# Fourier tokens folded four ways, with the small token transform as one block before the first group's attention

## The chip, the cores and the metric

The kernel runs on one core of one Trainium2 chip. The metric is the device time of one execution in microseconds (us). Engines are PE (matmuls), DVE (vector), ACT (scalar), POOL (GpSimd) and SP (its queue issues loads). All data is float32.

## The reference, cut to what matters

One encoder layer on 1,024 tokens of 1,024 channels: layer norm, an input projection, then attention (8 heads) and a Fourier branch merged by sigmoid gates, an output projection, and a retrieval layer (PEER) that fetches 128 rows of each of two large tables for every token. The change touches the Fourier branch:

```python
zf = z.astype(jnp.float32).reshape(B, S, F_GROUPS, F_GROUP_DIM)
y = jnp.fft.fft2(zf, axes=(1, 3), norm='ortho').real
return y.astype(z.dtype).reshape(B, S, F_DIM) @ w_fourier
```

The real part is, for each of 4 groups, cos(tokens) times cos(channels) minus sin(tokens) times sin(channels), applied to z of 1,024 tokens by 128 channels.

## The kernel before, in words

The program is one straight list of instructions per engine, tied by semaphores written out by hand. A front end first makes, for all 1,024 tokens, the normalised rows (`h0_done`), their transposes, the latents (L374), the Fourier input `zT` (L383, evicted by ACT at L1007), the rotary key (L393), the keys (L414) and values (L422), and the transposed retrieval keys. Then the tokens go in 4 groups of 256. Each group has a front part, `front(g, m)`, a table of 256 steps m: 16 attention units (2 query tiles times 8 heads, one every 5 steps), gates (from m = 85), the output projection, a layer norm, 16 query products and the choice of experts; and a retrieval part, bound to the gathered rows. The front part of group 0 runs alone, before any row is gathered (`gather_u` waits for `handed`, which the choice of experts sets); that of groups 1 to 3 runs beside the retrieval of the group before. The order within a step is the order of the calls in the loops at the end of each engine's program.

An attention unit u on PE is: for the first query tile, the head's query product (L470, at m = 5u), which ACT copies (L1042) and DVE rotates (L760 to L763); the scores (L488, 5u+2) into `fA`; DVE's row maximum (L768); ACT's exponential (L1047); 8 transposes (L344, 5u+6), copied by DVE (L776); and the value products (L506, 5u+9). The scores of unit u+1 wait until the exponential of unit u has read `fA`.

The Fourier branch before is done so. `zc`: for 8 token tiles and 4 groups one product with [cos | -sin] of the channels, 128x256 each (L405), evicted in turn by DVE (L722) and ACT (L1014) into `zcs`; the column k = 512 of the token transform is made apart, as a sum over tiles (L726) times alternating signs (L440, `y_mid`). The token transform uses that the outputs k and 1024-k share their products, so 512 columns are made: `dft(m)`, called at each step of `front(0, m)`, issues at every odd m below 64 two 128x512 products (L598), accumulated over 8 token tiles in `acc`, with a 512 KB piece of the matrix `dft_seq` streamed through a ring of 4 by ACT's queue (L1029, L1136). After each 8 of them DVE joins the halves (L928 to L932) and ACT spills the result (L1141).

```python
            for m in range(STEPS):
                if has_slot(-1, m + LEAD, False):
                    peer(-1, m + LEAD)
                front(0, m)
                dft(m)
```

## Time and profile before

| | |
|---|---|
| runs | 3511.56 us median of 3 (3509.41 to 3511.76) |
| profiled execution | 3506.43 us, its span 3504.6 us |
| PE busy | 2694.9 us, 77% of the span |
| DVE, ACT, POOL busy | 2224.8, 1631.8, 2170.5 us |
| DMA | 1240.83 MB, mean 354 GB/s |
| chain that ended last | POOL 26%, DMA 26%, PE 16%, DVE 11%, issue 11% |

The shares are means over two different programs in one: a front end and a first group without gathers, up to about 610 us, and the retrieval after it, in which the DMA row of the page stands at 9 tenths and about 400 GB/s throughout. In rows that list time by order, the number in brackets is the idle time of the engine before the row and what ended it. An fp32 matmul is two instructions in the trace: `x4` for a pair of 128x512 products.

### The profile page before, as it was taken

Reading aid. Unit: us, or ns where it says so; the run is one execution under the profiler, and the core shown is the slowest. Engines: PE = TensorE matmul, PEld = TensorE weight load, DVE = VectorE, ACT = ScalarE, POOL = GpSimd, SP = SyncE. Lnnn points to the kernel's source line nnn. Section 1 sums busy time; section 2 is a strip of 40 time slices with the busy share of each in tenths; the row PEclk is TensorE's granted clock in tenths of the full one; section 3 lists DMA queues with packets and bytes.
Section 4 is the critical chain, followed back from the end, with each engine's and each line's share of the span. In section 5 each row is a group of like instructions: output and inputs, shape, how many; then the busy total and the mean of one; then the engine's idle time right before and its main releaser. Section 6 shows DMA issues by size and latency. Waiting matters only on the chain.

```text
span 3504.6 us, 40872 instructions
## 1 busy us (share of the span) xinstructions
PE 2694.9 (77%) x14008; PEld 2139.5 (61%) x14008; DVE 2224.8 (63%) x5012; ACT 1631.8 (47%) x1852; POOL 2170.5 (62%) x2075
## 2 busy tenths in 40 slices
PE   6999986677788777687887777777887777766676
PEld 3455755566676666576775666666766665555555
DVE  5143218668766678578766677677666785567753
ACT  1121102466554555465545555565555454445445
POOL 4000003777777766777777767777777667777775
PEclk9999998689899898789899986898998885566656
DMA  4224437999999999999999999999999999999998
GB/s 173 100 78 156 150 114 248 406 399 399 382 410 409 409 409 387 392 402 361 406 409 409 406 408 389 393 398 373 409 409 408 409 379 409 409 409 409 409 407 319
DMA packets 350433, 1240.83 MB, mean 354 GB/s; under 512 B 38481, under 2 KB 46161, under 8 KB 349713
## 3 DMA queue, kind: packets, MB, share of 16 engines
q0 software_dynamic: 294912, 1073.87, 77.9%
q1 hardware_dynamic: 34096, 117.94, 9.1%
q10 hardware_dynamic: 21216, 46.40, 3.7%
q8 instruction: 111, 1.82, 0.2%
q14 instruction: 98, 0.79, 0.1%
HBM read 1222.33 MB, written 15.73 MB: 353 GB/s over the span
## 4 chain that ended last, share of the span: by engine, by line
POOL 26%; DMA 26%; PE 16%; DVE 11%; issue 11%; DVEq 7%; ACT 3%; SPq 0%; ACTq 0%; POOLq 0%
POOL rows L322 14%; DMA rows<-in_peer_u,ids_peer 13%; POOL rows L313 13%; DMA rows<-in_peer_v,ids_peer 12%; DVE rows L889 3%; PE fA L530 2%; ACT av L1116 2%; PE mB L374 2%; PE acc L598 2%; PE acc L609 1%; PE fB L542 1%; PE mB L506 1%; PE fA L488 1%; DVEq L834 1%; DVEq L745 1%
## 5 line engine op out<-in xcount | busy, mean ns | idle before, releaser
L609 PE MATMUL acc<-ident,av 128*128 128x128 f32 x8192 | 1394.7, 328 | 683.6 <-ACT av L1116 672.0
L1116 ACT ACTIVATE av<-rows,coef 128x1024 f32<-128x1024 f32 x1024 | 1172.1, 1146 | 1298.8 <-DMA rows<-in_peer_v,ids_peer 1194.4
L609 PEld LDWEIGHTS acc<-ident,av 128*128 128x128 f32 x8192 | 1155.3, 170 | 938.7 <-ACT av L1116 881.2
L313 POOL DMA_INDIRECT rows<-in_peer_u,ids_peer x1024 | 1034.3, 1010 | 830.8 <-DVE ids_peer L860 353.0
L322 POOL DMA_INDIRECT rows<-in_peer_v,ids_peer x1024 | 1088.1, 1063 | 339.6 <-issue 257.2
L889 DVE CUSTOM_DVE_ANT_0 rows<-rows,fB 128x1024 f32<-128x1024 f32 x538 | 650.2, 1215 | 386.6 <-DMA rows<-in_peer_u,ids_peer 382.7
L889 DVE CUSTOM_DVE_ANT_0 rows<-rows,hh 128x1024 f32<-128x1024 f32 x486 | 590.9, 1222 | 329.6 <-DMA rows<-in_peer_u,ids_peer 323.1
L576 PE MATMUL mB<-hT_g,wring 128*128 128x256 f32 x1024 | 253.9, 405 | 1.1 <-ACT hT_g L1078 1.1
L530 PE MATMUL fA<-hT_g,wring 128*128 128x256 f32 x1024 | 237.7, 388 | 0.0
L576 PEld LDWEIGHTS mB<-hT_g,wring 128*128 128x128 f32 x1024 | 206.6, 207 | 31.1 <-ACT hT_g L1078 1.5
L530 PEld LDWEIGHTS fA<-hT_g,wring 128*128 128x128 f32 x1024 | 196.4, 196 | 25.9
L506 PEld LDWEIGHTS mB<-V,S 128*128 128x128 f32 x1024 | 139.1, 216 | 11.8 <-DVE S L776 6.1
L506 PE MATMUL mB<-V,S 128*128 128x64 f32 x1024 | 140.1, 297 | 3.5 <-DVE S L776 3.5
L488 PE MATMUL fA<-KT,hT_g 96*128 96x512 f32 x256 | 123.8, 606 | 4.9 <-issue 2.8
L1047 ACT ACTIVATE S<-fA,small 128x1024 f32<-128x1024 f32 x64 | 71.0, 1109 | 107.5 <-DVE small L770 76.9
L542 PE MATMUL fB<-yo,wring 128*128 128x256 f32 x512 | 115.8, 379 | 0.0
L1107 ACT ACT_TABLE_LOAD x83 | 106.5, 1283 | 1.5
L542 PEld LDWEIGHTS fB<-yo,wring 128*128 128x128 f32 x512 | 95.4, 190 | 12.0
L776 DVE COPY S<-fB 128x1024 f32<-128x1024 f32 x64 | 78.1, 1221 | 37.2 <-PE fB L344 36.0
L768 DVE TENSOR_REDUCE small<-fA 128x1 f32<-128x1024 f32 x64 | 78.1, 1220 | 22.1 <-PE fA L488 21.9
L889 DVE DVE_READ_ACCUMULATOR2_ANT dots<- 128x1 f32 x1024 | 84.1, 82 | 0.0
L344 PE MATMUL fB<-ident,S 128*128 128x128 f32 x512 | 80.4, 309 | 4.1 <-ACT S L1047 4.1
(158 smaller groups left out, 2130.3 us busy)
## 6 DMA issues: line engine op xcount, KB each, us to landing
wring<-in_wstream SPq DMA_DIRECT2D x192, 512.0 KB, 6.8
ln<-in_dft_seq ACTq DMA_DIRECT2D x32, 512.0 KB, 3.5
rows<-in_peer_u,ids_peer POOLq DMA_INDIRECT x1024, 11.1
rows<-in_peer_v,ids_peer POOLq DMA_INDIRECT x1024, 11.2
hT_g<-in_x SPq DMA_DIRECT2D x8, 512.0 KB, 3.7
hres_spill<-KT ACTq DMA_DIRECT2D x8, 512.0 KB, 2.7
hT_spill<-rows ACTq DMA_DIRECT2D x1, 4096.0 KB, 11.1
wring<-in_wstream SPq DMA_DIRECT2D x16, 256.0 KB, 6.1
```

Of the source, the lines that this page charges most:

```text
L313: pool.indirect_dma_start(u_rows[:, ring(g, i, NU), :], None, peer_u, bass.IndirectOffsetOnAxis(ap=ids_peer[:, t, s:s + 1], axis=0)).then_ ...
L322: pool.indirect_dma_start(v_rows[:, ring(g, i, NV), :], None, peer_v, bass.IndirectOffsetOnAxis(ap=ids_peer[:, t, s:s + 1], axis=0)).then_ ...
L344: return nc.tensor.transpose(out_, in_, ident[:, :])
L488: last = mm(fA[:, half * 512:(half + 1) * 512], qT_g[0:QK, h, tok(qt)], KT[0:QK, h, half * 512:(half + 1) * 512], start=True, stop=True)
L506: last = mm(m1[:, h * VD:(h + 1) * VD], probsT[:, tok(k)], V[:, k, h * VD:(h + 1) * VD], start=k == 0, stop=k == TT - 1)
L530: last = mm(gb[:, j * GROUP:(j + 1) * GROUP], w[:, tok(k)], hT_g[:, k, :], start=k == 0, stop=k == KD - 1)
L542: last = mm(yb[:, j * GROUP:(j + 1) * GROUP], w[:, tok(4 * j + k)], src[:, k, :], start=k == 0, stop=k == 3)
L576: last = mm(m0[:, (qc % 2) * GROUP:(qc % 2 + 1) * GROUP], w[:, tok(k)], hT_g[:, k, :], start=k == 0, stop=k == KD - 1)
L609: last = mm(acc[:, tok(k)], av[:, i % NAV, tok(k)], ident[:, :], is_transpose=True, start=i % SLOTS == 0 and k % 4 == 0, stop=i % SLOTS == ...
L889: v.tensor_tensor_reduce(out=row, in0=row, in1=h1, scale=1.0, scalar=0.0, op0=ALU.mult, op1=ALU.add, accum_out=dots[:, b, i % BATCH:i % BA ...
L1107: s.activation(act_out[:, k % 2, :], dots[:, k % 2, :], ACT.Gelu).then_inc(act_done, 1)
L1116: s.activation(av[:, i % NAV, :], v_rows[:, ring(g, i, NV), :], ACT.Copy, scale=coef[:, b, i % BATCH:i % BATCH + 1]).then_inc(scaled, 1)
```

## The change

The 1,024 tokens are folded four ways by symmetry: DVE adds and subtracts z at t and 1024-t, then at t and 512-t, so that four vectors of 256 tokens are left (even and odd outputs, cosine and sine). The channel products are then 32 of 128x128 (L408 after) instead of 32 of 128x256, and the token transform needs 8 products of 128x255 to 257 per group, plus one of a single row for token 256 (`mid_row`, L607 after), instead of 16 of 128x512. The matrix `dft_mat` is 1 MB, loaded once at the start by SP's queue; the 16 MB of `dft_seq` are no longer streamed. The transform is no longer called in the steps of the first group's attention but as a block ahead of it, with `acc` and `fA` in turn as output; ACT copies the sine part, DVE writes the four quarters of the output with strides of 2 and -2. PE waits for the last of them (`y_done`) before the attention, and ACT issues the loads of `ln` and waits for the spill (`y_spilled`) before its part of it.

```diff
@@ -146,11 +145,14 @@
         hT_all = rows[:, 0:KD, :]
-        zcs = hT_all.rearrange("p t (g c) -> p t g c", g=FG)
+        zcs = rows[:, KD:KD + 4, :].rearrange("p a (b n) -> p (a b) n", b=2)
         zT = hh
+        fold = S2[:, :, :, :].rearrange("p t c n -> p (t c n)").rearrange("p (g n) -> p g n", g=FG)
+        zx = hh.rearrange("p g (x n) -> p g x n", x=4)
...
-        dft_ring = ln[:, :, :].rearrange("p r (m n) -> p r m n", m=2)
+        dft_sb = ln[:, 2:4, :]
+        mid_sgn, mid_row = yo[0:1, 0, 0:EVEN], yo[0:1, 0, 512:1024]
...
-        cos_part, sin_part = acc[:, 0:512], acc[:, 512:1024]
+        dft_ps = (acc, fA)
...
             load(w_uv_sb, w_uv, w_kv_in)
             load(rope_all[64:128, :], rope_tab, rope_in)
+            load(dft_sb, dft_mat.rearrange("(h p) n -> p h n", p=P), dft_in)
...
@@ -394,15 +395,24 @@
 
-            for n in range(TT * FG):
-                tt, g = divmod(n, FG)
+            for n in range(2 * FG):
+                g, pair = divmod(n, 2)
+                pe.wait_ge(folded, g + 1)
                 if n == 0:
-                    pe.wait_ge(hT_in, 16)
-                if g == 0 or n == 0:
                     pe.wait_ge(z_sb, 2 * FG)
                 if positive(n - 3):
-                    pe.wait_ge(zc_sb[n % 2], n // 2 - 1)
-                mm(banks[n % 4][:, 0:2 * FD], zT[:, g, tok(tt)], dftc, start=True, stop=True).then_inc(zc_ps, 1)
+                    pe.wait_ge(zc_sb[n % 2], (n - 4) // 2 + 1)
+                for x in range(2):
+                    for half in range(2):
+                        o = (2 * x + half) * FD
+                        last = mm(banks[n % 4][:, o:o + FD], zx[:, g, 2 * pair + x, tok(half)],
+                                  dftc[:, pair * FD:(pair + 1) * FD], start=True, stop=True)
+                last.then_inc(zc_ps, 1)
+            pe.wait_ge(zc_sb[0], 3)
+            for g in range(FG):
+                last = mm(banks[0][0:1, g * FD:(g + 1) * FD], fold[:, g, HALFK:HALFK + 1], dftc[:, 0:FD],
+                          start=True, stop=True)
+            last.then_inc(zc_ps, 1)
 
             pe.wait_ge(w_kv_in, 32)
...
@@ -433,14 +443,9 @@
-            for e in range(2):
-                pe.wait_ge(zc_sb[e], TT * FG // 2)
-            pe.wait_ge(z_sum, 1)
-            for g in range(FG):
-                last = mm(m0[:, g:g + 1], zsum[:, g, :], altern[:, 0:1], start=True, stop=True)
-            last.then_inc(y_mid, 1)
-            pe.wait_ge(y_mid, 2)
-
+            pe.wait_ge(zc_sb[0], FG + 1)
+            pe.wait_ge(zc_sb[1], FG)
+            pe.wait_ge(dft_in, 16)
 
             def chunk(g, c):
...
@@ -587,16 +592,19 @@
             def dft(m):
 
-
-                if m % 2 == 1 and m < 2 * TT * FG:
-                    n = m // 2
-                    g, tt = divmod(n, TT)
-                    if tt == 0 and g > 0:
-                        pe.wait_ge(y_done, g)
-                    pe.wait_ge(dft_in[n % NDFT], 16 * (n // NDFT + 1))
-                    for cs, part in enumerate((cos_part, sin_part)):
-                        last = mm(part, zcs[:, tt, g, cs * FD:(cs + 1) * FD], dft_ring[:, n % NDFT, cs, :],
-                                  start=tt == 0, stop=tt == TT - 1)
+                g, step = divmod(m, DFT_PERIOD)
+                if g < FG and step == 1:
+                    if g > 1:
+                        pe.wait_ge(y_done, g - 1)
+                    ps_g = dft_ps[g % 2]
+                    for x, (first, count) in enumerate(((0, EVEN), (512, HALFK), (EVEN, HALFK - 1), (512 + HALFK, HALFK))):
+                        cols = slice(first, first + count)
+                        for half in range(2):
+                            o = (2 * (x % 2) + half) * FD
+                            last = mm(ps_g[:, cols], zcs[:, 2 * g + x // 2, o:o + FD], dft_sb[:, half, cols],
+                                      start=half == 0, stop=half == 1 and x > 0)
+                        if x == 0:
+                            mm(ps_g[:, cols], mid_row[:, g * FD:(g + 1) * FD], mid_sgn, start=False, stop=True)
                     last.then_inc(dft_used, 1)
...
+            for m in range(DFT_PERIOD * FG):
+                dft(m)
+            pe.wait_ge(y_done, FG)
             for m in range(STEPS):
                 if has_slot(-1, m + LEAD, False):
                     peer(-1, m + LEAD)
                 front(0, m)
-                dft(m)
             for g in range(GROUPS):
                 for m in range(STEPS):
...
@@ -698,6 +708,21 @@
             latents(TT - 1)
+
+            for g in range(FG):
+                dve.wait_ge(z_sb, 2 * g + 2)
+                z, a, b = zT[:, g, :], fold[:, g, 0:S // 2 + 1], fold[:, g, S // 2:S]
+                v.tensor_copy(a[:, 0:S // 2 + 1:S // 2], z[:, 0:S // 2 + 1:S // 2])
+                v.tensor_tensor(a[:, 1:S // 2], z[:, 1:S // 2], z[:, S - 1:S // 2:-1], ALU.add)
+                v.tensor_tensor(b[:, 1:S // 2], z[:, 1:S // 2], z[:, S - 1:S // 2:-1], ALU.subtract)
+                dve.drain()
+                v.tensor_tensor(zx[:, g, 0, :], a[:, 0:HALFK], a[:, S // 2:HALFK:-1], ALU.add)
+                v.tensor_tensor(zx[:, g, 1, :], a[:, 0:HALFK], a[:, S // 2:HALFK:-1], ALU.subtract)
+                v.tensor_tensor(zx[:, g, 2, 0:1], b[:, HALFK:HALFK + 1], b[:, HALFK:HALFK + 1], ALU.subtract)
+                v.tensor_tensor(zx[:, g, 2, 1:HALFK], b[:, 1:HALFK], b[:, S // 2 - 1:HALFK:-1], ALU.subtract)
+                v.tensor_copy(zx[:, g, 3, 0:1], b[:, HALFK:HALFK + 1])
+                v.tensor_tensor(zx[:, g, 3, 1:HALFK], b[:, 1:HALFK], b[:, S // 2 - 1:HALFK:-1],
+                                ALU.add).then_inc(folded, 1)
 
...
+            for n in range(0, 2 * FG, 2):
                 dve.wait_ge(zc_ps, n + 1)
-                v.tensor_copy(zcs[:, tt, g, :], banks[n % 4][:, 0:2 * FD]).then_inc(zc_sb[0], 1)
-
-            dve.wait_ge(zc_sb[0], TT * FG // 2)
-            dve.wait_ge(zc_sb[1], TT * FG // 2)
-            v.reduce_sum(zsum, zcs[:, :, :, 0:FD].rearrange("p t g c -> p g c t"), AX).then_inc(z_sum, 1)
+                v.tensor_copy(zcs[:, n, :], banks[n % 4]).then_inc(zc_sb[0], 1)
+            dve.wait_ge(zc_ps, 2 * FG + 1)
+            v.tensor_copy(mid_row, banks[0][0:1, :]).then_inc(zc_sb[0], 1)
             dve.wait_ge(stored, 16)
             for i in range(TT):
...
@@ -919,26 +938,30 @@
             def dft(m):
 
-                if m % (2 * TT) == 2 * TT - 1 and m < 2 * TT * FG:
-                    g = m // (2 * TT)
-                    dve.wait_ge(dft_used, TT * (g + 1))
+                g, step = divmod(m, DFT_PERIOD)
+                if g < FG and step == 3:
+                    dve.wait_ge(sin_sb, g + 1)
                     if g >= 2:
                         dve.wait_ge(y_spilled[g % 2], 16)
                     y = y_part[:, g % 2, :]
-                    v.tensor_copy(y[:, S // 2:S // 2 + 1], ymid[:, g:g + 1])
-                    v.tensor_copy(ybuf[:, 0:512], sin_part)
+                    cos_even, cos_odd = dft_ps[g % 2][:, 0:EVEN], dft_ps[g % 2][:, 512:512 + HALFK]
+                    even, odd = cos_even[:, 1:HALFK], cos_odd
+                    sin_g = ybuf[:, 512 * (g % 2):512 * (g % 2 + 1)]
+                    sin_even, sin_odd = sin_g[:, 1:HALFK], sin_g[:, HALFK:2 * HALFK]
+                    v.tensor_copy(y[:, 0:S // 2 + 1:S // 2], cos_even[:, 0:EVEN:HALFK])
+                    v.tensor_tensor(y[:, 2:S // 2:2], even, sin_even, ALU.add)
+                    v.tensor_tensor(y[:, S - 2:S // 2:-2], even, sin_even, ALU.subtract)
+                    v.tensor_tensor(y[:, 1:S // 2:2], odd, sin_odd, ALU.add)
+                    v.tensor_tensor(y[:, S - 1:S // 2:-2], odd, sin_odd, ALU.subtract).then_inc(y_done, 1)
                     dve.drain()
-                    v.tensor_tensor(y[:, 0:512], cos_part, ybuf[:, 0:512], ALU.add)
-                    v.tensor_tensor(y[:, S - 1:S // 2:-1], cos_part[:, 1:512], ybuf[:, 1:512],
-                                    ALU.subtract).then_inc(y_done, 1)
-                    dve.drain()
-
+
+            for m in range(DFT_PERIOD * FG):
+                dft(m)
             for m in range(STEPS):
                 if m == L0:
                     dve.wait_ge(ln_in, 64)
                 peer(-1, m, False)
                 front(0, m)
-                dft(m)
 
             def group(g, last):
...
@@ -1008,10 +1031,9 @@
             load_queries(0)
-            for n in range(1, TT * FG, 2):
-                tt, g = divmod(n, FG)
+            for n in range(1, 2 * FG, 2):
                 act.wait_ge(zc_ps, n + 1)
-                s.activation(zcs[:, tt, g, :], banks[n % 4][:, 0:2 * FD], ACT.Copy).then_inc(zc_sb[1], 1)
+                s.activation(zcs[:, n, :], banks[n % 4], ACT.Copy).then_inc(zc_sb[1], 1)
             act.wait_ge(kr_sb, 2)
             for n in range(H):
...
-            for n in range(NDFT):
-                act.dma_start(dft_ring[:, n, :, :],
-                              dft_seq[:, tok(n), :].rearrange("m p n -> p m n")).then_inc(dft_in[n], 16)
 
 
...
 
             def dft(m):
-                n = m // 2 - 1 + NDFT
-                if m % 2 == 0 and NDFT <= n < TT * FG:
-                    act.wait_ge(dft_used, n - NDFT + 1)
-                    act.dma_start(dft_ring[:, n % NDFT, :, :],
-                                  dft_seq[:, tok(n % TT), :].rearrange("m p n -> p m n")).then_inc(dft_in[n % NDFT], 16)
-                if m % (2 * TT) == 1 and 0 < m // (2 * TT) <= FG:
-                    g = m // (2 * TT) - 1
+                g, step = divmod(m, DFT_PERIOD)
+                if g < FG and step == 2:
+                    act.wait_ge(dft_used, g + 1)
+                    if g > 1:
+                        act.wait_ge(y_done, g - 1)
+                    sin_g = ybuf[:, 512 * (g % 2):512 * (g % 2 + 1)]
+                    sin_both = dft_ps[g % 2][:, :].rearrange("p (b n) -> p b n", b=2)[:, :, HALFK:512]
+                    s.activation(sin_g.rearrange("p (b n) -> p b n", b=2), sin_both, ACT.Copy).then_inc(sin_sb, 1)
+                if g < FG and step == 4:
                     act.wait_ge(y_done, g + 1)
                     act.dma_start(yT_d[:, g, :], y_part[:, g % 2, :]).then_inc(y_spilled[g % 2], 16)
-                if m == 2 * TT * FG + 2:
+                if m == DFT_PERIOD * FG:
                     for j in range(4):
...
 
+            for m in range(DFT_PERIOD * FG + 1):
+                dft(m)
             for m in range(STEPS):
                 if has_slot(-1, m + LEAD, False):
                     scale(-1, m + LEAD)
                 gelus(-1, m, False)
...
     rope = np.concatenate([cos, cos, -sin, sin]).astype(np.float32)
-    n = np.arange(S)
-    w = 2 * math.pi * ((n[:, None] * n[None, :]) % S) / S
-    dft_seq = np.stack([np.cos(w), np.sin(w)])[:, :, :S // 2].astype(np.float32)
+    n = np.arange(S // 4)
+    even, odd = np.arange(0, S // 2 + 1, 2), np.arange(1, S // 2, 2)
+
+    def turn(rows, cols):
+
+        return 2 * math.pi * ((rows[:, None] * cols[None, :]) % S) / S
+
+    sin_rows = np.r_[S // 4, 1:S // 4]
+    dft_mat = np.concatenate([np.cos(turn(n, even)), np.sin(turn(n, even[1:-1])), np.cos(turn(n, odd)),
+                              np.sin(turn(sin_rows, odd))], axis=1).astype(np.float32)
+    mid_sign = np.cos(turn(np.array([S // 4]), even)).astype(np.float32)
     c = np.arange(FD)
```

On PE, between the channel products and the second attention unit, the order before is (the name `hh` holds z, `keysT` the latents, `ln` the transform's matrix):

```order
L405 MATMUL fA<-av,hh 128x256 x2
L405 MATMUL fB<-av,hh 128x256 x2
L414 MATMUL mB<-keysT,ln 128x512 x16
L422 MATMUL mB<-ln,keysT 128x512 x16
L344 MATMUL mB<-ident,hT_g 128x128 x16
L440 MATMUL mB<-small,prod 128x1 x4
L470 MATMUL mB<-cqT_g,wring 128x256 x2
L598 MATMUL acc<-ln,rows 128x512 x2
L488 MATMUL fA<-KT,hT_g 128x512 x2
L598 MATMUL acc<-ln,rows 128x512 x2
L470 MATMUL mB<-cqT_g,wring 128x256 x2
L598 MATMUL acc<-ln,rows 128x512 x2
```

and of the change:

```order
L413 MATMUL fA<-av,S 1x128 x4
L424 MATMUL mB<-keysT,ln 128x512 x16
L432 MATMUL mB<-ln,keysT 128x512 x16
L345 MATMUL mB<-ident,hT_g 128x128 x16
L604 MATMUL acc<-ln,rows 128x257 x2
L607 MATMUL acc<-yo 128x257
L604 MATMUL acc<-ln,rows 128x256 x2
L604 MATMUL acc<-ln,rows 128x255 x2
L604 MATMUL acc<-ln,rows 128x256 x2
L604 MATMUL fA<-ln,rows 128x257 x2
```

The 32 pairs at L598 no longer lie between the attention's instructions; after the block (four times the last rows, on `acc` and `fA` in turn) L475, the query product, follows, and then scores, query product, transposes, scores and value products without anything between.

On ACT, at the end of the block, with the semaphores that it waits for, the order of the change is:

```order
L1159 ACTIVATE ybuf<-fA 128x512 [waits y_done,dft_used]
L1162 DMA yT_spill<-hh 128x1024 [waits y_done]
L1165 DMA ln<-in_lnp 128x1024 x4
L1061 ACTIVATE hT_g<-mB 64x256 [waits q_ps,y_spilled1,y_spilled0]
L1066 ACT_TABLE_LOAD
L1066 ACTIVATE S,rowsum<-fA,small 128x1024 [waits row_max]
```

The spill and the four `ln` loads now stand ahead of the first query copy (L1061), which waits for the spills. Before, they came at m = 65 and 66, behind 13 units.

## Rows read from the trace of the kernel before

**Rows 1.** Busy time by stage: stretch, length, busy us of each engine (instructions), clock, DMA, GB/s
```profile
235.00:358.00 123.00, 117.82 (x504) 71.54 (x504) 50.53 (x77) 20.07 (x35) 0.00 (x0) 0.99 0.45 150
358.00:378.00 20.00, 15.39 (x91) 11.69 (x88) 9.03 (x10) 3.61 (x6) 0.00 (x0) 0.91 0.81 261
378.00:510.00 132.00, 119.89 (x483) 92.61 (x482) 20.55 (x34) 12.00 (x23) 0.00 (x0) 0.94 0.42 128
...
620.00:3504.00 2884.00, 2172.46 (x12016) 1804.68 (x12013) 1977.23 (x4453) 1527.97 (x1642) 2085.68 (x2011) 0.82 1.01 398
```

**Rows 2.** Chain of work that ended last, 230 to 237 us: start, us, what
```profile
230.98 1.07 PE mB L440 x8
232.28 1.13 PE mB L470 x4
...
235.13 1.78 PE fA L488 x4
```

**Rows 3.** Order of time on PE: start, us, instruction, count, idle before it
```profile
182.25 1.13 PE L405 MATMUL fA<-av,hh 128*128 128x256 f32 x4
...
185.31 1.10 PE L405 MATMUL fA<-av,hh 128*128 128x256 f32 x4 [1.06 <-DVE rows L722]
...
197.47 13.90 PE L414 MATMUL mB<-keysT,ln 128*128 128x512 f32 x32
```

**Rows 4.** Order of time on PE, the last attention units of group 0
```profile
363.92 1.88 PE L488 MATMUL fA<-KT,hT_g 96*128 96x512 f32 x4
365.63 1.90 PE L506 MATMUL mB<-V,S 128*128 128x64 f32 x16
368.59 1.09 PE L344 MATMUL fB<-ident,S 128*128 128x128 f32 x8 [1.06 <-ACT S L1047]
369.51 1.88 PE L488 MATMUL fA<-KT,hT_g 96*128 96x512 f32 x4
...
374.18 1.93 PE L344 MATMUL fB<-ident,S 128*128 128x128 f32 x8 [1.05 <-ACT S L1047]
377.42 3.67 PE L506 MATMUL mB<-V,S 128*128 128x64 f32 x16 [1.31 <-DVE S L776]
```

**Rows 5.** Groups by line and shape, 235 to 358 us
```profile
L598 PE MATMUL acc<-ln,rows 128*128 128x512 f32 x125 | 60.2, 603 | 1.6 <-DVE hh L932 1.1 <-issue 0.5
```

**Rows 6.** Order of time on DVE, 28 to 251 us
```profile
28.28 1.29 DVE L646 BATCH_NORM_STATS2 st<-hT_g 128x6 f32<-128x512 f32 x2 [2.13 <-DMA hT_g<-in_x]
...
31.68 0.69 DVE L671 TENSOR_TENSOR V<-mB,KT 128x512 f32<-128x512 f32 x1 [1.59 <-PE mB L374]
...
175.59 0.75 DVE L711 SCALAR_TENSOR_TENSOR prod<-mB,small,yo 32x512 f32<-32x512 f32 x1 [62.80 <-PE mB L393]
...
184.73 0.42 DVE L722 COPY rows<-fA 128x256 f32<-128x256 f32 x1
...
198.15 7.22 DVE L726 TENSOR_REDUCE prod<-rows 128x512 f32<-128x4096 f32 x1 [0.49 <-ACT rows L1014]
...
249.92 0.42 DVE L760 TENSOR_TENSOR prod<-mB,rope_g 32x256 f32<-32x256 f32 x1 [4.63 <-PE mB L470]
...
250.86 0.42 DVE L763 TENSOR_TENSOR hT_g<-prod 32x256 f32<-32x256 f32 x1
```

**Rows 7.** Order of time on ACT and its queue
```profile
168.49 0.69 ACT L1007 ACTIVATE hh<-fB,small 128x512 f32<-128x512 f32 x1 [6.18 <-PE fB L383]
...
357.92 0.34 ACTq L1141 DMA_DIRECT2D yT_spill<-hh  x1
358.30 2.28 ACTq L1144 DMA_DIRECT2D ln<-in_lnp  x4
```

**Rows 8.** DMA issues, 160 to 400 us: KB each, median us to landing
```profile
yT_spill<-hh ACTq DMA_DIRECT2D x4, 512.0 KB, 2.9
```

**Rows 9.** Order of time on PE, scores after the first join of a Fourier group
```profile
264.50 3.22 PE L488 MATMUL fA<-KT,hT_g 96*128 96x512 f32 x4 [2.83 <-issue]
```

**Rows 10.** Busy time and clock of a 2 us stretch (columns as in rows 1)
```profile
382.00:384.00 2.00, 2.00 (x7) 1.55 (x6) 0.10 (x1) 0.00 (x0) 0.00 (x0) 0.50 0.00 0
```

25 lines of the change are left out of this document (8 added, 17 removed).

## The prediction

> **What bounds the kernel now.** I read the stages first [rows 1]. From 620 us on, DMA is busy 1.01 of the time at 398 GB/s: that is the retrieval, which the change does not touch. Its first gathers need the expert numbers at the end of the first group's front part, so whatever that front part gains should arrive at the end of the kernel as an earlier start of the same 2,884 us. From 235 to 358 us PE is busy 117.8 of 123.0 us, from 378 to 510 us 119.9 of 132.0, and DVE and ACT never come near: the front end is PE's. The chain of waits agrees; around the start of the attention it runs over PE and the small round trip for column 512 [rows 2]. So a PE instruction taken away before 358 us is time, as far as nothing else becomes the limit there. That limit can be read: from 358 us on the Fourier products are over, and units run bare. Scores start at 363.92 and again at 369.51 [rows 4]: 5.59 us per unit, with PE idle 1.06 us in each, until ACT's exponential is done. This is a chain of scores, row maximum, exponential and transposes, and it is the floor for an attention without other work.
>
> **The change part by part.** Every item is a shift of the time at which something starts.
>
> 1. *1 MB more at the start.* `dft_mat` goes ahead of the third x tile on SP's queue. At 398 GB/s [rows 1] it is 2.6 us. DVE was idle 2.13 us for that tile until 28.28, took its statistics until 30.09, and was idle 1.59 us until PE's product was ready at 31.68 [rows 6]. So 2.6 less 1.59 is left: **+1.1** (0 to +2.6).
>
> 2. *The folds on DVE.* Per group two operations of 511 columns at 0.69, four of 256 at 0.42 (durations of copies of 512 and 256 columns [rows 6, 7]), three tiny ones of 0.15: 3.5 us. The last part of z is evicted at 168.49 [rows 7]; DVE is idle 62.8 us until 175.59 [rows 6]. The last fold ends near 173, before the rotary work, which comes next on DVE, and before PE's channel products at 182.25. **0**. If that cover were gone, 3.5 us of the last group would show.
>
> 3. *Channel products.* Before, 32 pairs of instructions from 182.25 to 197.47, 15.2 us, of which 1.06 a wait for DVE's first copy [rows 3]: (15.2 - 1.06) / 64 = 0.22 us for 256 columns. After, 64 instructions of 128 columns. No such product is in the trace; bounds are the same 0.22 (14.1 us) and the value products, whose 16 instructions with 128 columns of weights and only 64 moving take 1.90 [rows 4], 0.12 or less. Half of 0.216 is 0.108; I take it, since it lies by that lower row: 6.9 us, and 0.9 for eight instructions of the single row. Copies of 512 columns (0.69, every second on ACT) fit into 0.86 us of PE per bank. The first wait goes too: with 4 banks of 0.86 us PE reaches the fifth only at 185.7, when DVE has copied the first. 15.2 - 7.8: **-7.4** (0 to -8).
>
> 4. *Column 512.* The sum over tiles, 7.22 us on DVE [rows 6], lay beside key products: 0. The round trip from 230.98 to 232.28 [rows 2] goes: **-1.3**.
>
> 5. *The block.* Per group 16 instructions of about 256 columns and two of the row product: 18 x 0.216 = 3.9, four times 15.5 us. PE waits for no one inside: the third group needs the first joined, 3.9 us later at the latest. DVE's third join waits for a spill: it is issued at about 7 us into the block, lands 2.9 later [rows 8], and is needed at 12.5. At the end all is bare: ACT's sine copy (0.69 and 0.2 to be released) and DVE's five operations (4 x 0.42, 0.15, 0.2), 2.9 us until PE may go on. Then ACT issues the spill (0.34) and four `ln` loads (2.28) [rows 7] and waits for the spill to land, 2.9 [rows 8], with 2 MB of `ln` behind it: 3.2. Behind that wait stands the first query copy (0.5 with its release), and PE's scores wait for it. From the block's start to the first scores: 15.5 + 2.9 + 3.2 + 0.6 = 22.2. Before, from 232.28 to 235.13 [rows 2], it was 2.8. **+19.4** (+17 to +24).
>
> 6. *The attention without the Fourier products.* They were 64 pairs of 128x512, 125 of their instructions seen at 60.2 us with overlapping ends [rows 5]. Scores of unit 0 to those of unit 15 took 235.13 to 369.51, 134.4 us. After, the eight units of the second query tile cost 5.6 each, with 0.65 once for the output's transposes. Units of the first tile also have the query product and the rope: after scores (1.72) PE does values (1.73) and the query product (four instructions at 0.216, 0.87), at 4.3; the rope runs from 0.2 later for 1.36 (249.92 to 250.86 + 0.42 [rows 6]); so scores can start at 5.95. Seven of these, 41.7, and 8 x 5.6 + 0.65 = 45.4: 87.1 us. **-47.3** (-35 if such a unit were 7.5).
>
> Sum at full clock: 1.1 - 7.4 - 1.3 + 19.4 - 47.3 = **-35.5**.
>
> 7. *The clock.* The trace shows the granted clock fall to 1.2 GHz where PE pauses: after 2.83 us of idle, scores took 3.22 instead of 1.88 [rows 4, 9]. It fell once more in the bare units: the transposes at 374.18 took 1.93 instead of 1.09, the values 3.67 instead of 1.90 [rows 4], and at 382 to 384 us it was still 0.50 with PE fully busy [rows 10]. That second fall cost about 4.4 us. Three bare units held full clock and then lost it. Now there are eight, and the block ends in 2.9 us of idle and about 3 more after the first query product. I reckon 2 us for a fall at the block's end and two or three falls at 2 to 4 us in the bare units, against one of 4.4 that was there and may come again: **+7** (-4 to +15).
>
> Together -28.5. Against the profiled execution's 3506.43 that is 3477.9; this execution was 5 us below the median of the runs, 3511.56, and I forecast for the median: **3483 us**.
>
> **The rivals.**
>
> *A. The clock holds.* The bare units stay at 2.4 GHz, as from 358 to 374 us, and the late fall may be missed: -35.5 to -40, 3474. Against it speaks that the fall came within three bare units.
>
> *B. The clock stays low: slower.* Place: the attention. PE was kept at full clock there by the Fourier products filling each gap; bare, it works 15.4 of 20.0 us [rows 1]. If it is granted 1.2 GHz all through, a unit is PE's own work at double time: scores 3.4, values 3.5, transposes 1.9, 8.8 instead of 5.6, and with the query product 10.5 instead of 5.95. 8 x 3.2 + 8 x 4.55 = 62 us, less 35.5: +26.5, 3538 us. It decides if the half clock covers over 57% of the stage. Against it: the first tile's units have hardly a gap, and at half clock the gaps close, and with the gate products, which leave none, the clock came back (0.94 over 378 to 510 us, though 0.50 at 382 [rows 1, 10]). The Trainium skill, "TensorE: Matmul & The Clock Gate", Part 4: PE-mode transpose, says that transposes do not count as PE being busy for the clock. By that rule a bare unit holds the clock less well than its busy time suggests, which would give this rival's time; the three units at full clock, each with transposes right before its scores, speak against its full form.
>
> *C. The rope units do not come down.* They have not been seen bare. If the query copy and rope push the maximum behind them on DVE and a unit stays near 7.5, 7 x 1.55 = 11 us less is gained: -17.5, 3494.
>
> *D. The start does not carry over.* If the retrieval made up the difference (it did not wait for the front end, but for bandwidth it would need anyway), the time stays at 3511. Against it: the first gather needs the first group's expert numbers, and up to 510 us DMA is busy under half of the time [rows 1], so bandwidth holds nothing back there.
>
> **How the numbers follow.** The forecast has 0.63, A 0.14, B 0.04, C 0.14, D 0.05. The predicted time is that of the forecast, 3483. The range goes from A's 3472 to 3500, which takes in C and the clock's upper bound; B and D and the tails stay out. A change under 0.2% (7 us) could not be told from none here. Faster 0.91, within 0.2% 0.05, slower 0.04.
>
> **What would show it.** The channel products should take 8 us and the key products start near 191; the block should start near 225 and hold PE 15.5 us; the first scores near 247 and the sixteenth near 334 at full clock, up to 342 with falls; scores to scores 5.6 in the second tile and 5.95 in the first. The retrieval should be as long as before. The forecast is wrong if the third x tile comes over 3 us later, if PE stalls inside the block, if a unit of the first tile is over 6.5 at full clock, or if 0.50 stands for the clock over most of the attention.

## The result and the profile after

Four runs of each kernel on one chip: 3468.1 us after (median; 3467.9 to 3475.5), 3510.5 us before. The ratio is 0.989, 95% interval 0.987 to 0.991: faster by 42 us, where 28.5 were forecast, and 4 us below the range's lower end. The profiled execution took 3468.17 us, its span is 3466.4; before they were 3506.43 and 3504.6. Two executions of the kernel before in a later batch, 3673 and 3691 us, were in the slower of the two states that its runs show and are left out of every mean below.

**The start.** On DVE, in order of time (start, us, line, operation, in brackets the idle time before it and its releaser), the third x tile now comes at 32.90 instead of 28.28, and its latents are made at 34.61 instead of 31.68 [rows 6]: 2.9 us later. Further on PE (last line, from its own order of time) needs 15.60 us for the first 32 instructions of the Fourier input, 13.90 before: the granted clock was half from 117.0 to 120.4.

```profile
32.90 1.29 DVE L656 BATCH_NORM_STATS2 st<-hT_g 128x6 f32<-128x512 f32 x2 [6.53 <-DMA hT_g<-in_x]
...
34.61 0.68 DVE L681 TENSOR_TENSOR V<-mB,KT 128x512 f32<-128x512 f32 x1
...
173.88 0.68 DVE L716 TENSOR_TENSOR S<-hh 128x511 f32<-128x511 f32 x1
...
175.24 0.43 DVE L719 TENSOR_TENSOR hh<-S 128x256 f32<-128x256 f32 x1
...
180.19 0.75 DVE L736 SCALAR_TENSOR_TENSOR prod<-mB,small,yo 32x512 f32<-32x512 f32 x1 [3.39 <-PE mB L394]
...
116.25 15.60 PE L384 MATMUL fA<-rows,wring 128*128 128x512 f32 x32
```

The folds of the last group lie at 173.8 to 176.8, and DVE is idle again until 180.19: they cost nothing.

**The channel products** on PE take from 186.85 to 195.16, 8.3 us, where they took 15.2 [rows 3]. 64 instructions of 128 columns are 7.3 of them, 0.115 us each; the eight of the single row are 1.0.

```profile
186.85 2.05 PE L408 MATMUL fA<-av,hh 128*128 128x128 f32 x16
...
194.19 1.03 PE L413 MATMUL fA<-av,S 128*1 128x128 f32 x8
195.16 2.41 PE L424 MATMUL mB<-keysT,ln 128*128 128x512 f32 x5
```

**The block and what stands behind it,** PE in order of time. A group is 4.27 to 4.38 us, and no instruction waits until the last has been issued. The block lies at 228.77 to 246.14.

```profile
228.77 1.13 PE L604 MATMUL acc<-ln,rows 128*128 128x257 f32 x4 [0.78 <-DVE keysT L755]
229.83 0.70 PE L607 MATMUL acc<-yo 1*128 1x257 f32 x2
230.46 2.85 PE L604 MATMUL acc<-ln,rows 128*128 128x256 f32 x12
233.15 1.03 PE L604 MATMUL fA<-ln,rows 128*128 128x257 f32 x4
...
243.29 2.85 PE L604 MATMUL fA<-ln,rows 128*128 128x256 f32 x12
248.34 1.13 PE L475 MATMUL mB<-cqT_g,wring 128*128 128x256 f32 x4 [2.20 <-DVE hh L955]
251.71 3.78 PE L493 MATMUL fA<-KT,hT_g 96*128 96x512 f32 x4 [2.24 <-ACT hT_g L1061]
```

On ACT and its sequencer at the same place: the sine copy, the spill, the four `ln` loads, then the first query copy, held by the spill.

```profile
246.18 0.60 ACT L1159 ACTIVATE ybuf<-fA 128x512 f32<-128x512 f32 x1 [3.68 <-PE fA L604]
248.32 0.33 ACTq L1162 DMA_DIRECT2D yT_spill<-hh  x1
248.68 2.28 ACTq L1165 DMA_DIRECT2D ln<-in_lnp  x4
251.28 0.38 ACT L1061 ACTIVATE hT_g<-mB 64x256 f32<-64x256 f32 x1 [4.51 <-DMA yT_spill<-hh]
```

**The attention,** PE in order of time, a unit of the first query tile and the last ones of the second. Scores to scores are 6.10 us in the first tile (265.24 to 271.34) and 5.60 in the second (335.44 to 341.04), as long as in the bare units before [rows 4].

```profile
265.24 1.96 PE L493 MATMUL fA<-KT,hT_g 96*128 96x512 f32 x4
267.03 1.90 PE L511 MATMUL mB<-V,S 128*128 128x64 f32 x16
268.76 1.08 PE L475 MATMUL mB<-cqT_g,wring 128*128 128x256 f32 x4
270.25 1.06 PE L345 MATMUL fB<-ident,S 128*128 128x128 f32 x8 [0.41 <-ACT S L1066]
271.34 1.96 PE L493 MATMUL fA<-KT,hT_g 96*128 96x512 f32 x4
...
335.44 1.88 PE L493 MATMUL fA<-KT,hT_g 96*128 96x512 f32 x4
...
340.11 1.09 PE L345 MATMUL fB<-ident,S 128*128 128x128 f32 x8 [1.05 <-ACT S L1066]
341.04 1.88 PE L493 MATMUL fA<-KT,hT_g 96*128 96x512 f32 x4
...
345.71 1.97 PE L345 MATMUL fB<-ident,S 128*128 128x128 f32 x8 [1.05 <-ACT S L1066]
```

Busy time by stretch (columns as in [rows 1]). In the attention PE is busy 83 of 100 us and the mean granted clock is 0.97 of 2.4 GHz: it is 1.2 GHz from 250.1 to 256.9 us, beside the first scores (3.78 us instead of 1.88), and then not until the transposes at 345.71. That is so in this execution; in the profiles of mat_late and after_pad, with the same attention, the clock fell twice more in the bare units, in mat_late from 318.9 to 322.3 and from 325.7 to 329.1 us. The last two rows are the kernel's remainder from the first gather, here and, in the second fence, in the kernel before:

```profile
245.00:345.00 100.00, 83.07 (x466) 59.77 (x464) 52.94 (x78) 23.69 (x42) 0.00 (x0) 0.97 0.18 64
345.00:358.00 13.00, 10.97 (x43) 9.64 (x44) 2.12 (x3) 0.66 (x2) 0.00 (x0) 0.61 0.34 111
...
516.00:3466.40 2950.40, 2197.21 (x12254) 1823.81 (x12253) 2045.17 (x4660) 1547.77 (x1675) 2131.50 (x2048) 0.83 1.01 397
```

```profile
544.60:3504.60 2960.00, 2220.47 (x12256) 1845.07 (x12254) 2044.53 (x4660) 1547.78 (x1675) 2122.49 (x2048) 0.82 1.01 396
```

POOL's first gather, whose start is the handover between the two parts, in order of time after and before:

```profile
516.07 1.35 POOL L314 DMA_INDIRECT rows<-in_peer_u,ids_peer  x1 [319.83 <-DVE ids_peer L879]
```

```profile
544.60 1.34 POOL L313 DMA_INDIRECT rows<-in_peer_u,ids_peer  x1 [352.96 <-DVE ids_peer L860]
```

The sixteenth unit's scores are at 341.04, before at 369.51 [rows 4]: 28.47 us earlier. The first gather is 28.53 us earlier. From there on the work is the same: DVE 4,660 instructions in 2,045 us and ACT 1,675 in 1,548 in both rows, 2,048 gathers in both. Yet it takes 2,950.4 instead of 2,960.0 us. So of the 38.3 us between the two profiled executions 28.5 are the front end, as forecast, and 9.6 come from a part that the change doesn't touch.

### The profile page after: what moved, and what is told of

The parts are those of the page before. It is cut to its first block, busy times and chain, and to the rows that moved or that the text cites. A ratio compares the mean times of both kernels' runs of the same rounds, so it can differ in the third digit from the quotient of the medians.

```text
span 3466.4 us, 40743 instructions
## 1 busy us (share of the span) xinstructions
PE 2633.6 (76%) x13952; PEld 2103.6 (61%) x13952; DVE 2224.2 (64%) x5039; ACT 1630.2 (47%) x1844; POOL 2179.5 (63%) x2075
## 4 chain that ended last, share of the span: by engine, by line
DMA 27%; POOL 25%; PE 14%; DVE 13%; issue 11%; DVEq 7%; ACT 3%; SPq 0%; ACTq 0%; POOLq 0%
POOL rows L314 13%; DMA rows<-in_peer_u,ids_peer 13%; POOL rows L323 12%; DMA rows<-in_peer_v,ids_peer 12%; DVE rows L908 3%; PE fA L535 2%; ACT av L1135 2%; PE acc L617 2%; PE mB L375 1%; PE fA L493 1%; PE fB L547 1%; DVEq L762 1%; DVEq L838 1%; DVEq L764 1%; DVEq L766 1%
## 5 line engine op out<-in xcount | busy, mean ns | idle before, releaser
L617 PE MATMUL acc<-ident,av 128*128 128x128 f32 x8192 | 1372.8, 324 | 696.0 <-ACT av L1135 685.7
L617 PEld LDWEIGHTS acc<-ident,av 128*128 128x128 f32 x8192 | 1136.8, 168 | 947.5 <-ACT av L1135 893.6
L314 POOL DMA_INDIRECT rows<-in_peer_u,ids_peer x1024 | 1085.8, 1060 | 790.4 <-DVE ids_peer L879 319.8
L323 POOL DMA_INDIRECT rows<-in_peer_v,ids_peer x1024 | 1045.7, 1021 | 329.6 <-issue 263.7
```

The source lines that it names most:

```text
L314: pool.indirect_dma_start(u_rows[:, ring(g, i, NU), :], None, peer_u, bass.IndirectOffsetOnAxis(ap=ids_peer[:, t, s:s + 1], axis=0)).then_ ...
L323: pool.indirect_dma_start(v_rows[:, ring(g, i, NV), :], None, peer_v, bass.IndirectOffsetOnAxis(ap=ids_peer[:, t, s:s + 1], axis=0)).then_ ...
L617: last = mm(acc[:, tok(k)], av[:, i % NAV, tok(k)], ident[:, :], is_transpose=True, start=i % SLOTS == 0 and k % 4 == 0, stop=i % SLOTS == ...
```

## The experiments

Eighteen runs of fourteen kernels in five batches. The kernel before took 3,509 us in one batch and 3,782 to 3,824 in the other four, so each is compared with the kernel before of its own batch. The profile gives the first gather; "rest" is the mean of all runs less that gather, and the column shows its difference to the mean of the kernel before in that batch less 544.6, its own first gather (the two variants of it with the same front end have 544.4 and 545.0), with standard errors of the means. The gather comes from one execution each, and these errors don't hold its scatter: the changed kernel alone has it at 516.1, 518.7 and 516.8, the kernel of extra_loads at 517.2, 513.2 and 514.7.

| run | before, median | this, median | ratio (95%) | first gather | rest less rest of before |
|---|---|---|---|---|---|
| after | 3510.5 | 3468.1 | 0.989 (0.987 to 0.991) | 516.1 | -9.9 ± 3.2 |
| after_again | 3823.6 | 3789.3 | 0.991 (0.988 to 0.993) | 518.7 | -9.4 ± 2.4 |
| after_pad | 3823.6 | 3791.4 | 0.991 (0.988 to 0.993) | 517.1 | -7.0 ± 3.0 |
| before_moved | 3823.6 | 3826.7 | 1.000 (0.999 to 1.001) | 545.0 | +0.1 ± 2.1 |
| spill_late | 3823.6 | 3794.1 | 0.992 (0.989 to 0.995) | 519.6 | -4.8 ± 2.7 |
| extra_loads | 3782.2 | 3747.2 | 0.991 (0.987 to 0.994) | 517.2 | -7.0 ± 5.1 |
| fold_in_steps | 3782.2 | 3751.6 | 0.991 (0.987 to 0.994) | 514.2 | -3.0 ± 3.1 |
| block_unfolded | 3782.2 | 3808.7 | 1.006 (1.004 to 1.008) | 568.9 | -1.6 ± 3.3 |
| spread | 3782.2 | 3731.6 | 0.986 (0.983 to 0.989) | 496.8 | -6.7 ± 3.5 |
| after_delayed | 3509.2 | 3502.3 | 0.998 (0.997 to 0.999) | 547.4 | -9.5 ± 1.2 |
| before_shifted | 3509.2 | 3509.3 | 1.000 (0.999 to 1.001) | 544.4 | +0.7 ± 1.1 |
| spread_ln_later | 3509.2 | 3450.6 | 0.984 (0.982 to 0.985) | 493.9 | -7.5 ± 1.7 |
| mat_late | 3509.2 | 3468.0 | 0.989 (0.987 to 0.990) | 513.3 | -9.9 ± 1.7 |
| sems_kept | 3784.2 | 3746.0 | 0.990 (0.988 to 0.992) | 515.5 | -7.5 ± 2.6 |
| extra_loads_again | 3784.2 | 3750.9 | 0.992 (0.990 to 0.993) | 513.2 | -2.2 ± 2.9 |
| before_sp_load | 3784.2 | 3785.4 | 1.000 (0.999 to 1.002) | 548.5 | -2.5 ± 2.7 |
| after_control | 3784.2 | 3748.3 | 0.991 (0.988 to 0.994) | 516.8 | -6.3 ± 6.0 |
| extra_loads_third | 3782.3 | 3754.3 | 0.993 (0.991 to 0.994) | 514.7 | -2.3 ± 3.4 |
| before_sp_load_again | 3782.3 | 3785.0 | 1.000 (0.998 to 1.001) | 554.2 | -9.5 ± 2.9 |

### Which half of the change gives the time

**fold_in_steps** keeps the fold and puts the small transform back between the attention's units, a group every 16 steps.

```diff
-DFT_PERIOD = 8
+DFT_PERIOD = 16
-        dft_ps = (acc, fA)
+        dft_ps = (acc, acc)
-            for m in range(DFT_PERIOD * FG):
-                dft(m)
-            pe.wait_ge(y_done, FG)
             for m in range(STEPS):
                 front(0, m)
+                dft(m)
```

> The fold alone: folded tokens and the small transform, but its products called from the steps of the first group's attention as before (a group's 18 instructions together at step 1, 17, 33, 49, all into acc). If the front end is set by PE's work and the unit's chain, the block's 15.5 us and the bare 5.5 us behind it go, and 3.9 us lumps in three units come, each partly in the unit's idle time: the first gather starts at about 506 us on the first chip, 10 us before the changed kernel's. If the lumps' joins hold up the chain (DVE's five operations and ACT's copy stand before the row maximum and the exponential), it comes at 511 or later. So the place would cost 5 to 10 us, and the fold be worth over 33. On the retrieval: theory F expects the changed kernel's.

**block_unfolded** is the other half: the kernel before, its 64 products of 128x512 unchanged but called as a block ahead of the attention.

```diff
+            for m in range(2 * TT * FG):
+                dft(m)
+            pe.wait_ge(y_done, FG)
             for m in range(STEPS):
                 front(0, m)
-                dft(m)
```

> The place alone: the kernel before with its unfolded transform as one block ahead of the first group's attention. 64 products of 128x512, 55 us, plus three joins of 2.9 us on which acc waits, plus the end's 5.5, against an attention that falls from 134.4 to about 90: the first gather at 565 us, 20 us after that of the kernel before. If the matrix ring cannot follow (512 KB per 1.72 us is 305 GB/s, landing in 3.5 us), it is later still, 575 or more. On the retrieval: theory F expects that of the kernel before.

The fold alone brings 30.6 us (3751.6 against 3782.2), its first gather lies at 514.2, 1.9 us ahead of the changed kernel's and within the scatter of that. The place alone costs 26.5 us, with the first gather 24 us later. PE in order of time shows both. First fold_in_steps, with a lump of 4.3 us between the scores and the values of a unit, and further on bare units at half clock:

```profile
251.96 1.95 PE L493 MATMUL fA<-KT,hT_g 96*128 96x512 f32 x4
253.75 1.03 PE L604 MATMUL acc<-ln,rows 128*128 128x257 f32 x4
254.71 0.70 PE L607 MATMUL acc<-yo 1*128 1x257 f32 x2
255.34 2.85 PE L604 MATMUL acc<-ln,rows 128*128 128x256 f32 x12
258.03 1.89 PE L511 MATMUL mB<-V,S 128*128 128x64 f32 x16
...
312.53 3.62 PE L493 MATMUL fA<-KT,hT_g 96*128 96x512 f32 x4
```

Then block_unfolded, where the block takes 66.6 us (232.47 to 299.06), a wait of 2.2 for DVE's joins after each group among them:

```profile
232.47 14.05 PE L598 MATMUL acc<-ln,rows 128*128 128x512 f32 x32 [0.25 <-DVE small L738]
248.74 14.00 PE L598 MATMUL acc<-ln,rows 128*128 128x512 f32 x32 [2.21 <-DVE hh L934]
...
299.06 1.35 PE L470 MATMUL mB<-cqT_g,wring 128*128 128x256 f32 x3 [2.21 <-DVE hh L934]
```

So the gain is the fold's. Placed as a block, products no longer fill the 1.05 us that PE waits for ACT's exponential in each bare unit; lumps hardly fill it either. In fold_in_steps the two lumps between units of the first tile cost their whole 4.3 us (scores to scores 10.4 instead of 6.1), the one in the second tile 3.1. The expected 506 us for the first gather was missed by 8: the clock was at half from 309.6 to 323.3 us, and three units there took 7.2, 8.4 and 6.8 us instead of 5.6 each, 5.6 more in all. So that the two places come out alike is partly the clock of this profile; at full clock the steps would have been the better place by 5 to 6 us, an estimate from these rows and those of the changed kernel.

### The terms of the front end

**spill_late** moves the `ln` loads and the wait for the spills back behind the units.

```diff
-                if m == DFT_PERIOD * FG:
-                    for j in range(4):
-                        act.dma_start(ln[:, j, :], lnp[3 + j:4 + j, :].to_broadcast([P, D])).then_inc(ln_in, 16)
-                    for i in range(2):
-                        act.wait_ge(y_spilled[i], 16 * (FG // 2))
...
                 front(0, m)
+                if m == 66:
+                    for j in range(4):
+                        act.dma_start(ln[:, j, :], lnp[3 + j:4 + j, :].to_broadcast([P, D])).then_inc(ln_in, 16)
+                    for i in range(2):
+                        act.wait_ge(y_spilled[i], 16 * (FG // 2))
```

> The changed kernel with the four ln loads and the wait for the spills put back to step 66 of the attention, where they were. In the changed kernel ACT's first query copy waits until 251.28, and PE's first scores start at 251.71, 3.2 us after the query product's 248.34; the clock falls at 250.1. Theory W (the wait is what it costs): scores start at 250.5, after the rope alone, 1.2 us earlier, and if the pause is then short enough for the clock to stay up, the first scores take 1.9 instead of 3.8 and the first gather starts 3 to 4 us earlier, at 512 to 513. Theory P (the pause before the query product is enough for the fall): the first gather moves by 1.2 us only, to 514.9.

Its PE, in order of time:

```profile
246.24 1.32 PE L475 MATMUL mB<-cqT_g,wring 128*128 128x256 f32 x4 [2.20 <-DVE hh L955]
249.10 3.75 PE L493 MATMUL fA<-KT,hT_g 96*128 96x512 f32 x4 [1.54 <-DVE hT_g L782]
```

From the query product to the scores it is 2.86 us instead of 3.37: ACT's wait for the spill was worth 0.5 us, since DVE's rope ends nearly as late. The scores still take 3.75. Here the clock falls at 247.0, right behind the pause of 2.2 us for the last join and before the second one, so ACT's wait isn't what it needs to fall. But such a pause doesn't always bring it down: in block_unfolded it came three times between groups of unbroken products, and only the group behind the second ran partly at half clock (15.70 us instead of 14.0). The first gather of spill_late was no earlier (519.6 against 518.7 in the same batch); this profile has further stretches of half clock in the attention.

**mat_late** loads the matrix behind the x tiles.

```diff
-            load(dft_sb, dft_mat.rearrange("(h p) n -> p h n", p=P), dft_in)
             for i in range(2, TT):
                 sp.wait_ge(h0_done, i - 1)
                 load(x_t[:, i % 2, :], x[tok(i), :], x_in[i % 2])
+            load(dft_sb, dft_mat.rearrange("(h p) n -> p h n", p=P), dft_in)
```

> The changed kernel with the 1 MB load of its matrix behind the x tiles on SP's queue. In the changed kernel DVE got the third x tile at 32.90 us instead of 28.28 and PE's product of the first tile waited for it: 2.93 us of shift, measured at L681 against L671. If the load is the cause, the tile comes at 28.3 to 29 again and the first gather 2 to 3 us earlier, at 513 to 514. If it only changes places with other loads, the gather stays at 516 to 518.

Its DVE, in order of time: the tile is back at 28.39, before 28.28 [rows 6], so 1 MB ahead of it on the queue costs it 4.5 us (in before_sp_load and before_sp_load_again, below, it came at 32.39 and 33.80).

```profile
28.39 1.29 DVE L656 BATCH_NORM_STATS2 st<-hT_g 128x6 f32<-128x512 f32 x2 [2.28 <-DMA hT_g<-in_x]
...
32.98 0.69 DVE L681 TENSOR_TENSOR V<-mB,KT 128x512 f32<-128x512 f32 x1 [2.79 <-PE mB L375]
```

The first gather moved 2.8 us forward, to 513.3, which is about the scatter between profiles of one kernel (516.1 to 518.7), so only the tile's delay is shown. The median stayed (3468.0, two runs; it is of another batch than 3468.1).

**spread** folds as the change does, loads the matrix behind the x tiles and cuts each group's products into four pieces, one every five steps of the attention, so that a piece lies in each unit.

```diff
-DFT_PERIOD = 8
+DFT_AT = (0, 3, 3) + tuple(range(10, 75, 5))
...
+                for i in range(4 * FG):
+                    if m == DFT_AT[i]:
+                        g, x = divmod(i, 4)
+                        if x == 0 and g > 0:
+                            pe.wait_ge(y_done, g)
```

> A version meant to beat both: the folded products of a group in four pieces, one piece (0.86 us, of 256 columns) per attention unit between the query product and the transposes of the unit before, where PE waits for the exponential, with two pieces in the first unit; the joins behind the row maximum; the matrix loaded after the x tiles; the ln loads and the wait for the spills at step 78. PE's idle 1.06 us in a bare unit takes a piece for nothing and so the clock should not fall there; units with a query product grow by about 0.6. Expected: the third x tile as in the kernel before, scores of unit 0 at 229, of unit 15 at 320, the first gather at 495, 21 us before the changed kernel's and 50 before that of the kernel before. If the pieces delay the transposes in every unit by their whole 0.86, it is 505.

It gained 50.6 us, with the first gather at 496.8. One wait was new, 3.86 us instead of 1.05 on PE before the last transposes; on ACT's sequencer the issue of the four `ln` loads, 3.53 us, stands ahead of the exponential. Both in order of time:

```profile
321.02 1.90 PE L511 MATMUL mB<-V,S 128*128 128x64 f32 x16
326.78 1.97 PE L345 MATMUL fB<-ident,S 128*128 128x128 f32 x8 [3.86 <-ACT S L1066]
```

```profile
321.81 3.53 ACTq L1165 DMA_DIRECT2D ln<-in_lnp  x4
325.52 1.11 ACT L1066 ACTIVATE S<-fA,small 128x1024 f32<-128x1024 f32 x1 [7.20 <-issue]
```

**spread_ln_later** issues those loads eight steps later and waits for the spills two steps later.

```diff
-                if m == 78:
-                    for j in range(4):
-                        act.dma_start(ln[:, j, :], lnp[3 + j:4 + j, :].to_broadcast([P, D])).then_inc(ln_in, 16)
+                if m == 80:
                     for i in range(2):
                         act.wait_ge(y_spilled[i], 16 * (FG // 2))
+                if m == 86:
+                    for j in range(4):
+                        act.dma_start(ln[:, j, :], lnp[3 + j:4 + j, :].to_broadcast([P, D])).then_inc(ln_in, 16)
```

> The spread version with the four ln loads at step 86 instead of 78. In its trace their issue took ACT's queue 3.53 us right before the last exponential, and PE was idle 3.86 us instead of 1.05 before the last transposes. They should be gone from there: the last transposes start 2.8 us earlier, the first gather at 494 instead of 496.8. If the loads only move the stall to the gates' sigmoid, which waits behind them on ACT from step 88, 1 us or less is gained.

It is the fastest of all, 3450.6 us: 58.7 below the kernel before in its batch, ratio 0.984 (0.982 to 0.985), where mat_late in that batch has 0.989. Its PE shows pieces of the transform where the waits for the exponential were, and the last transposes in time and at full clock:

```profile
236.65 1.08 PE L475 MATMUL mB<-cqT_g,wring 128*128 128x256 f32 x4
237.57 1.03 PE L604 MATMUL acc<-ln,rows 128*128 128x256 f32 x4
238.43 1.04 PE L345 MATMUL fB<-ident,S 128*128 128x128 f32 x8
239.31 1.88 PE L493 MATMUL fA<-KT,hT_g 96*128 96x512 f32 x4
...
325.92 1.09 PE L345 MATMUL fB<-ident,S 128*128 128x128 f32 x8 [1.05 <-ACT S L1066]
```

### Why the remainder is shorter

**after_again** asks first whether it is there in another batch, **after_control** asks it once more; both are the changed kernel as it is.

> The changed kernel once more, for its spread. In its first trace the first gather starts at 516.1 us instead of 544.6, 28.5 earlier, and from there to the end it takes 2950.3 us instead of 2960.0, 9.7 less. Theory S (spread): the 9.7 us is the spread of the retrieval between executions; over more executions the retrieval of both kernels has the same mean, the first gather stays at 516.1, and the time comes to 28 to 33 us under that of before. Theory M (memory): the retrieval is shorter for a lasting reason, where the two gathered tables and the spills lie in device memory (the inputs ahead of them are 3 MB smaller); then the difference stays at 36 to 42 us.

> The changed kernel as it is, as the yardstick for the three beside it: first gather at 516 to 519 us, ratio 0.989 on a chip of 3510 us, 0.990 on a slower one, from first gather to end about 9 us shorter than before.

It was: -9.4 ± 2.4, and -6.3 ± 6.0, which alone shows nothing.

**after_pad** gives the matrix the 4 MB of `dft_seq` in memory (one line, zeros appended; only the first 256 rows are loaded); **before_moved** declares `dft_seq` as the last input.

```diff
-        "dft_mat": dft_mat,
+        "dft_mat": np.concatenate([dft_mat, np.zeros((S - S // 4, S), np.float32)]),
```

> The changed kernel with its matrix input filled up with zeros to the 4 MB that the old one had, so that every other input lies where it lay before; only the first 1 MB is loaded, and nothing else is changed. Theory M expects the retrieval back at 2960 us, so 8 to 10 us slower than the changed kernel, with the first gather still at 516.1. Theory S expects the same time as the changed kernel, within its spread.

> The kernel before with its 4 MB matrix as the last of the inputs instead of the one between the identity and the channel matrix; the same instructions. Theory M expects a change of the retrieval, by up to 10 us faster, if what matters is what lies ahead of the small inputs or the output. Theory S expects no difference: first gather at 544.6, time as before within 0.2%.

Neither changes its kernel's time: after_pad is 0.7 ± 2.9 us above after_again, where 8 to 10 were expected, and before_moved 0.5 ± 2.1 above the kernel before. So the matrix's size and its place in the list of inputs aren't it. The two gathered tables stand ahead of the matrix in that list in every kernel, not behind it as the expectations of after_again take it, and no run records an address, so where the tables and the spills lie in memory is not shown.

**after_delayed** puts 32 products that nobody reads behind the block, which brings the first gather back to where it was before. **before_shifted** puts 16, 27 and 8 empty instructions into PE's, DVE's and ACT's programs.

```diff
             pe.wait_ge(y_done, FG)
+            for i in range(16):
+                for half in range(2):
+                    last = mm(fA[:, half * 512:(half + 1) * 512], zcs[:, i % 8, 0:FD], dft_sb[:, half, 0:512], start=True, stop=True)
+            last.then_inc(dft_used, 1)
```

> The changed kernel with 16 pairs of 128x512 products that nobody reads behind its block, about 27.5 us of PE, so that its first gather comes at 544 us, where the kernel before has it. It asks two things at once. Does a microsecond of the front end arrive whole at the end: the total should then be 27 to 29 us over the changed kernel's. And where do the further 5 to 9 us come from, by which the retrieval of the folded kernels was shorter: theory T (the retrieval runs slower by where it falls in time) expects the total of the kernel before, within 3 us; theory F (something that the folded program itself brings, whenever the retrieval starts) expects it 5 to 9 us below the kernel before.

> The kernel before with 16 empty instructions at the head of PE's program, 27 of DVE's and 8 of ACT's, which moves every later instruction in the programs by as much as the change moves DVE's; no work is changed. Theory A (the position of the retrieval's instructions, and so when they are fetched, makes the 5 to 9 us) expects the retrieval to change by several us. Otherwise it stays within 3 us of the kernel before, with the first gather at 545 to 546.

Busy time from the first gather to the end, first of after_delayed, then of before_shifted:

```profile
547.40:3496.90 2949.50, 2201.93 (x12254) 1827.27 (x12252) 2045.73 (x4660) 1548.43 (x1675) 2123.71 (x2048) 0.83 1.01 397
```

```profile
544.40:3505.00 2960.60, 2207.11 (x12256) 1831.61 (x12254) 2045.46 (x4660) 1547.96 (x1675) 2133.07 (x2048) 0.83 1.01 396
```

With its first gather 2.8 us later than that of the kernel before, the changed kernel still ends 7 us earlier (0.998, 0.997 to 0.999). So the shorter remainder is not a matter of when it starts. before_shifted shows that 16, 27 and 8 more instructions make no difference; of these only DVE's number is the change's own (5,012 and 5,039 instructions in the two profiles), while PE has 56 fewer with the change and ACT 8 fewer, its dropped loads not counted. So the positions that the change gives on PE and ACT weren't tested. And against mat_late in the same batch a first gather that is 34.1 us later (547.4, 513.3) means an end that is 34.3 us later (3502.3, 3468.0): the start carries over whole.

**extra_loads**, run three times, adds 32 loads of 512 KB on ACT's queue to the changed kernel; **before_sp_load**, run twice, adds one load of 1 MB on SP's queue to the kernel before, at the place of the matrix; **sems_kept** adds unused semaphores to the changed kernel, so that the others have their numbers of before.

```diff
+                for j in range(4):
+                    if n > 0:
+                        act.wait_ge(extra_in[j], 16 * n)
+                    act.dma_start(rows[:, KD + j, :].rearrange("p (m n) -> p m n", m=2),
+                                  dft_mat[:, (j % 2) * 512:(j % 2) * 512 + 512].rearrange("(m p) n -> p m n", m=2)
+                                  ).then_inc(extra_in[j], 16)
```

```diff
             load(rope_all[64:128, :], rope_tab, rope_in)
+            load(ln[:, 2:4, :], x[0:2 * P, :].rearrange("(h p) n -> p h n", p=P), spare_in)
```

> The changed kernel, with 32 loads of 512 KB in rows of 2 KB put on ACT's queue again (four after each eviction of z, into the rows that the channel products take later), as many and as large as those of the matrix ring that the change removed. Their 16 MB fall in a stretch in which DMA is nearly idle. So far the retrieval is 7 to 10 us shorter with the change, on two chips, and filling up the input did not bring it back. Theory Q (the queue: what the 32 loads leave behind, in its ring or in instructions to be fetched, slows the retrieval) expects the retrieval of the kernel before, 7 to 10 us longer than that of the changed kernel, with the first gather moved by less than 3 us. Theory F (it comes with the folded code in another way, or it is spread) expects the retrieval of the changed kernel.

> The same kernel as extra_loads, 32 loads of 512 KB on ACT's queue before the attention, on a chip where I hope for less scatter. If the history of that queue lengthens the retrieval of the kernel before, the time after the first gather is 9 us longer than after_control's. If not, equal within 2 us.

> The same kernel as extra_loads. On a chip where before takes 3510 us: time after the first gather 2964 us if the history of ACT's queue is the cause, 2955 if not. On one of 3784 us it tells only to 3 us.

> The kernel before with one more load of 1 MB (rows of x, read by nobody) on SP's queue ahead of the third x tile, where the changed kernel loads its matrix. The x tile should come 2 to 3 us later, and the first gather 3 to 4 us later (548). If the history of SP's queue is what shortens the retrieval, that falls by 9 us and the whole is 5 us shorter than before, ratio 0.9985; if not, the whole is 3 to 4 us longer, ratio 1.001.

> The same kernel as before_sp_load. On a chip where before takes 3510 us: first gather at 548.5, and after it 2955 us (whole 3504) if the history of SP's queue is the cause, 2964 (whole 3513) if not.

> The changed kernel with four unused semaphores (three in place of the matrix's ring, one after y_done), so that every later semaphore has the number that it has in the kernel before. Nothing is computed otherwise. If the semaphores' numbers make the folded retrieval shorter, the time from the first gather to the end returns to that of the kernel before, about 9 us longer than after_control, and the ratio to before goes to 0.992. If not, it is after_control's within 2 us, ratio 0.989.

The numbers of the semaphores are unlikely: the remainder stays 7.5 ± 2.6 us short. The queues stay undecided. These two batches and that of extra_loads were of the 3,782 to 3,784 us kind, whose remainder scatters too much. The three values of extra_loads together are -3.0 ± 2.0, between nothing and what the folded kernels show there without these loads (fold_in_steps, spread, sems_kept and after_control together: -6.0 ± 1.7). Unfolded kernels come out low there too: block_unfolded -1.6 ± 3.3, before_sp_load -2.5 ± 2.7 and -9.5 ± 2.9. The whole time of before_sp_load, both runs together, is 0.8 ± 1.9 us above that of the kernel before; with the 3.9 us by which its first gather came late in one profile, no effect would have given +3.9 and the full one about -6; its other profile had the gather 5.7 us later still, so its rest is known to some us only.

## Why the prediction was right and where it failed

The forecast's terms, against the traces of the profiled executions, each as a shift of PE's work:

| step | forecast | measured | from |
|---|---|---|---|
| 1, x tile, up to the channel products | +1.1 | +4.6 | L405 at 182.25, L408 at 186.85 |
| 2, folds | 0 | 0 | DVE idle 3.39 behind them |
| 3, channel products | -7.4 | -6.9 | 15.2, 8.3 |
| 4, column 512 | -1.3 | -1.3 | the round trip is gone |
| 5, block, until the first scores | +19.4 | +20.1 | 22.9 (228.77 to 251.71), before 2.8 |
| 6, attention | -47.3 | -45.0 | 89.3 (251.71 to 341.04), before 134.4 |
| 7, clock | +7 | within the rows above, about +3 | 1.7 in row 1, 1.4 in row 6 (first unit 7.5 instead of 6.1) |
| to the sixteenth scores | -28.5 | -28.5 | 341.04, 369.51 |
| from the first gather on | 0 | -9.6 | 2950.4, 2960.0 |

**What failed** is the last row. The text said that the gain "should arrive at the end of the kernel as an earlier start of the same 2,884 us", and among the marks "The retrieval should be as long as before". The front end came out at the number summed, and the retrieval was 9.6 us shorter. In each of the 14 folded runs the remainder is shorter than that of the kernel before; in the 3,782 to 3,784 us batches that says little, since the unfolded kernels are low there as well, but elsewhere it parts them: -4.8 to -9.9 folded, +0.1 and +0.7 unfolded. In the two batches of the 3,509 us kind, profiled executions alone: 2950.3, 2949.5, 2951.3 and 2953.9 us (after, after_delayed, mat_late, spread_ln_later) against 2960.0 and 2960.6 (before, before_shifted). The range had been built for the errors of the front end's terms; it gave the retrieval none, although the three runs of the kernel before already lay 2.4 us apart, and the profiled execution 5 us from their median. Two thirds of the miss of 15 us (3483 less 3468) is this; the rest is that 5 us, which the forecast added because the execution of before was below its median, while that of the changed kernel was at its own.

That the front end gave -28.5 us to the tenth is luck. The start cost 3.5 us more than forecast, the channel products gained 0.5 less, the block cost 0.7 more and the attention gained 2.3 less, 7.0 together, which took the place of the 7 us put down for the clock; of these 7.0 the falls that came are about 3.

The cause isn't known. The starts of the gathers from the first table, 256 to a group, counted in each profile from its first one, tell where the difference accrues. At gather 320 the changed kernel is 0.7 us behind the kernel before and after_delayed 0.2, so nothing is gained beside the front part of group 1. It comes beside the front parts of groups 2 and 3: 3.8 and 4.3 us ahead at gather 384, 8.1 and 10.5 at gather 768. In the last group, which has no front part beside it, no more is gained until its last gather, and 1 to 3 us behind that (before_shifted, for the scatter: 2.1 behind, 1.2 ahead, 0.8 behind, and 1.0 gained at the end). The median durations of single instructions in the costly groups are the same within 5 ns in six profiles of the 3,509 us kind. Shown not to be it: the time of the start, and the matrix's size and place among the inputs. The semaphores' numbers and a shift of the programs as before_shifted makes it are unlikely. Open are the history of the two DMA queues, the instructions' positions on PE and ACT, the addresses in memory, and the unfolded transform's place, since block_unfolded ran in a batch that can't tell.

**The single terms.** Step 1 was mis-sized: 1 MB ahead of the tile delays it by 4.5 us, where 2.6 were taken from the bandwidth of the retrieval; behind the wait of 1.59 for PE, 2.9 are left. The remaining 1.7 us up to the channel products are the stretch of half clock at 117.0 to 120.4, which isn't in the profile before nor in that of mat_late. Step 3 was right in choosing the lower bound: half the columns take about half the time (0.115 against 0.22). Step 5 forecast 15.5 us of products and measured 17.4: the two instructions with one row of weights take 0.63 us, where 0.43 were forecast, and the others 0.224 to 0.265 each instead of 0.216. It made up for 1.1 of that at the block's end, where the spill's landing was nearly hidden behind the rope. Step 6: a unit of the first tile is 6.10 us, not 5.95, and 5.60 of the second as read; the first of all, at half clock, is 7.5. Step 7 put a fall at the block's end and two or three in the bare units into the sum. In this execution there was the first and none of the others; the fall in the last units came late, at 345.7, and had been there before. In mat_late and after_pad there were two in the bare units as well, in spill_late more, so their number differs between profiles of the same attention.

**The rivals.** A, the clock holds: in this execution it held from 256.9 to 345.7 us, over fifteen units' scores, eight of them without a query product; in the other profiles named it didn't. Its time of 3474 was the nearest, though not for its reason, since the sum stayed at -28.5. B, the clock stays low: excluded; the granted clock is 0.97 in the stretch. The Trainium skill, "TensorE: Matmul & The Clock Gate", Part 4: PE-mode transpose, says that the full clock doesn't engage for transposes, which don't count as PE being busy in the same way. The trace doesn't bear it out here: each of the units of the second tile has 1.09 us of transposes in 5.60, and waits 1.05 before them, and the transposes at 340.11 still took 1.09 us, little more than half of the 1.97 at 345.71 at half clock. How much transposes count no run here separates. C, the rope units don't come down: they came to 6.10, a fraction of it. D, the start doesn't carry over: it carries over whole, as after_delayed shows against mat_late (34.1 us at the first gather, 34.3 at the end).

## What to carry to other kernels

A forecast that ends at a handover needs an allowance for what lies behind it, even if the code there is the same: read the scatter of that part in repeated runs, and give the range at least that. When work is cut to a quarter, look again for its best place: products that filled gaps by their mass do so no longer as a block or in lumps, and small pieces laid into the waits for the exponential were worth 17 us more than the block (3450.6 against 3468.0 of mat_late in the same batch, the matrix loaded late in both). Ahead of a tile that an engine waits for, a load that isn't needed soon cost its transfer and more here. And one profile of a stretch with pauses is one draw of the clock: compare several before a difference of 2 to 6 us is put down to the change.

## What the runs showed of the hardware

- 1 MB in front of a 512 KB tile on the same queue delayed the tile by 4.5 us (32.90 against 28.39), though 1 MB at the retrieval's 400 GB/s is 2.6. With another 1 MB load in the same place it came at 32.39 and 33.80 (before_sp_load and its repeat).
- An fp32 product with one row of weights and 257 columns took 0.63 us for its two instructions (229.83 to 230.46), dearer than two of 128 rows (0.45, a sixth of the 2.69 us from 230.46 to 233.15).
- A pause of 2.2 us after 17 us of unbroken products was followed by half clock (spill_late, from 247.0 us, scores 3.75 us); of four such pauses behind 14 to 16 us of products in block_unfolded two were (from 265.3 and from 299.4), two were not. Waits of 0.3 to 1.2 us in each unit were not followed by it for the 88.8 us from 256.9 to 345.7 in the changed kernel, but the fall at 345.7 came behind the same waits, and in mat_late so did two more, at 318.9 and 325.7.
- Issuing the same four broadcast loads took ACT's sequencer about 1.8 (fold_in_steps), 2.28 (after), 2.57 (spread_ln_later) or 3.53 us (spread), and in spread PE waited 2.8 us longer for the exponential behind them (3.86 instead of 1.05).
- The same kernel before took 3,509 us in one batch and 3,782 to 3,824 in others, once both on the same chip (3509.2 and 3784.2). The difference lies behind the first gather: in before_moved, at 3,827 us, that stayed at 545.0, and the rest moved 357 GB/s instead of 396.
